# Middle pairs of two feed-forward blocks computed column by token, without transposes of the gated values

## The chip, the cores and the metric

The program runs on one core of one Trainium2 chip. The metric is the device time of one execution in microseconds. Three runs of the kernel before gave 1178.71, 1179.95 and 1180.96 us, median 1179.95. Engines are called by their names: TensorE (PE in the profile), its weight loads (PEld), VectorE (DVE), ScalarE (ACT), GpSimd (POOL) and SyncE (SP, which issues the loads of weights).

## The reference, cut to what matters

256 tokens with 1024 features pass through one hybrid layer (feed-forward, attentions, feed-forward) and then two layers whose norms are modulated by a condition vector. There are four feed-forward blocks, called ffn0 to ffn3 in the kernel; ffn2 and ffn3 belong to the last two layers. All is float32.

```
def swiglu_2(h, w_gate, w_up, w_down):
    return (jax.nn.silu(h @ w_gate) * (h @ w_up)) @ w_down      # 1024 -> 2816 -> 1024

def second_block(...):
    cond = jax.nn.silu(c)
    for i in range(2):
        mod = (cond @ ada_w[i] + ada_b[i])[:, None, :]           # 1024 -> 6 x 1024
        sh1, sc1, g1, sh2, sc2, g2 = jnp.split(mod, 6, axis=-1)
        h = rmsnorm_2(x, norm1_g[i]) * (1.0 + sc1) + sh1
        y = ...attention of layer i...
        x = x + g1 * y
        h = rmsnorm_2(x, norm2_g[i]) * (1.0 + sc2) + sh2
        x = x + g2 * swiglu_2(h, w_gate[i], w_up[i], w_down[i])
    return x
```

## The kernel before

**Precision.** Each float32 matrix is split into a high part (rounded to the type float32r) and a low part (the rest), and each product is three matmuls: high by high, low by high, high by low. ScalarE makes the high part of a weight unit (`hi(u)`, a copy of 128 x 2048), VectorE the low part (`lo(u)`, a subtraction of the same size). The same is done for activations: `h_hi_t` and `h_lo_t` hold the normed input, feature by token, `hid_hi` and `hid_lo` the gated values.

**Weights.** They come in units of 1 MB through a ring of seven slots (`SLOT`, `HELD`); SyncE issues the load of a unit when `unit_done` says that the slot's last user is through. `hi` and `lo` of a unit are issued AHEAD = 4 units before TensorE uses it.

**A feed-forward block.** The 2816 hidden columns are taken in 11 pairs of 256 columns (`PAIRS`). A pair has three units: two for gate and up (part 0 and part 1, four 128-row chunks each, 256 gate columns beside 256 up columns) and one for down. In the kernel before, `gate_up(p, part, t)` keeps 128 tokens of the activations as TensorE's weights and streams 512 columns (gate and up together), so a result is token by column in bank 0 or 1 (`gu_bank`), for t = 0 and 1. ScalarE takes the silu of the gate half (`silu`), VectorE multiplies by the up half (`hidden`). The gated values are then token by column, but the down matmul wants them column by token, so `turn_hid` transposes them (four transposes of 128 x 128 a pair into bank 2), ScalarE copies the high part out of bank 2 (`hid_hi_of`) and VectorE subtracts the low part (`hid_lo_of`). `down_all(p)` adds 24 matmuls of 512 columns to the accumulators in banks 4 to 7. TensorE's order in pair p is: gate and up part 0, transposes of pair p - 1, gate and up part 1, down of pair p - 1, modulation job.

**Modulation.** While the feed-forward blocks run, VectorE also computes the vectors `cond @ ada_w`: one step (`ada(k)`, 128 x 1024) for each of 96 pieces that GpSimd loads, four steps in each of the pairs 2 to 9 of ffn0 to ffn2. The first step of a vector is a plain product. When a vector is complete, a modulation job (`MOD_JOBS`, one half vector a job) sums it over partitions: TensorE transposes it (or multiplies it by ones, for a gate vector, after a split into `acc_hi` and `acc_lo`) into **bank 3**, and VectorE reads bank 3 (`mod_job`, which raises `mod_read`). Jobs stand in pairs 2 to 9 of ffn2 and in pairs 2 and 3 of ffn3. VectorE does its part of the job as the last thing in its pair.

**Order.** Nothing is scheduled by a planner: each engine's instruction list is written by hand in the function `pair` and around it, each engine works through its list in order, and they meet at semaphores. Around the seventh norm (before ffn3) ScalarE's list is: `hi(v0 + 5)`, `hi(v0 + 6)`, then `norm_root(7, 0)`, which squares x of the first 128 tokens and takes the root; VectorE then scales x (`xn`) and TensorE turns it.

Of the kernel before, what the change touches and what calls it, by code (L numbers as in the profile page):

```python
# [6 lines left out]
F32 = mybir.dt.float32  # L7
# [6 lines left out]
P = 128  # L14
# [154 lines left out]

PASS = 4  # L170
# [15 lines left out]
def program(nc, inp, out):  # L186
    with ExitStack() as ctx:
# [12 lines left out]
        h_hi_t = sb("h_hi_t", [P, C, T], F32R)  # L200
        h_lo_t = sb("h_lo_t", [P, C, T], F32R)
# [102 lines left out]
        gu0_done, silu_done, hid_done = sem("gu0_done"), sem("silu_done"), sem("hid_done")  # L304
        hidT_done, hidhi_done, hidlo_done = sem("hidT_done"), sem("hidhi_done"), sem("hidlo_done")
# [34 lines left out]
        def hidT_count(f, p):  # L340

            return (PAIRS + 1) * f + p

# [96 lines left out]
        def _(act):  # L440
# [80 lines left out]
            def ffn(f, n, then):  # L521
# [15 lines left out]
                def hid_hi_of(p, cols, count):  # L537
                    act.wait_ge(hidT_done, count)
                    act.activation(hid_hi[:, p % 2, cols], ps[:, 2, cols], ACT.Copy).then_inc(hidhi_done, 1)  # L539

                def pair(p):
                    ug, ud = ffn_gate(f, p), ffn_down(f, p - 1)
                    if p > 0:
                        hid_hi_of(p - 1, slice(0, 2 * T), hidT_count(f, p - 1) + 1)
                    hi(ug + AHEAD)
                    silu(p, 0)
                    silu(p, 1)
                    hi(ug + 1 + AHEAD)
                    q = gate_of_pair(f * PAIRS + p)
                    if q is not None:  # L550
                        act.wait_ge(ada_used, C * (q + 1))
                        act.activation(acc_hi[:, :], ada_acc[:, q % 2, :], ACT.Copy).then_inc(acc_hi_done, 1)
                    if p > 0:
                        hi(ud + AHEAD)

                u0 = BASE[f"ffn{f}"]
                if f == 0:
                    silu(0, 0)
                    silu(0, 1)
                    hi(3)  # L560
                    act.wait_ge(cond_in, 16)
                    act.activation(cond[:, :], cond[:, :], ACT.Silu).then_inc(cond_ready, 1)
                    hi(4)
                    hi(5)
                    pair(1)
                    late_inputs()
                else:
                    silu(0, 0)
# [7 lines left out]
                    hid_hi_of(0, slice(0, 2 * T), hidT_count(f, 0) + 1)  # L576
                    silu(1, 1)
                    hi(u0 + 3 + AHEAD)
                    hi(u0 + 4 + AHEAD)
                for p in range(2, PAIRS - 1):  # L580
                    pair(p)
# [4 lines left out]
                hid_hi_of(p - 1, slice(0, 2 * T), hidT_count(f, p - 1) + 1)  # L586
                hi(end)
                silu(p, 0)
                hid_hi_of(p, slice(0, T), hidT_count(f, p) + 1)
# [15 lines left out]
                hid_hi_of(p, slice(T, 2 * T), hidT_count(f, p) + 2)  # L605
# [96 lines left out]
            def stick():  # L702
# [110 lines left out]
                hi(v0 + 5)  # L813
                hi(v0 + 6)
                norm_root(7, 0)
# [249 lines left out]
        def _(dve):  # L1065
# [145 lines left out]
            def ffn(f, n, then, factor=None, gated=None):  # L1211
                late = f < 2

                def hidden(p, t):
# [6 lines left out]
                    if p > 1:  # L1221
                        dve.wait_ge(hidT_done, hidT_count(f, p - 2) + 1)
# [15 lines left out]

                def pair(p):
# [9 lines left out]
                    q = gate_of_pair(f * PAIRS + p)  # L1249
                    if q is not None:  # L1250
                        dve.wait_ge(acc_hi_done, GATES.index(q) + 1)
                        V.tensor_tensor(acc_lo[:, :], ada_acc[:, q % 2, :], acc_hi[:, :].bitcast(F32), ALU.subtract) \
                            .then_inc(acc_lo_done, 1)
# [25 lines left out]
                else:  # L1279
# [10 lines left out]
                    lo(u0 + 3 + AHEAD)  # L1290
                    lo(u0 + 4 + AHEAD)
                for p in range(2, PAIRS - 1):
                    pair(p)
# [4 lines left out]
                hid_lo_of(p - 1, slice(0, 2 * T), hidT_count(f, p - 1) + 1)  # L1298
# [532 lines left out]
        def _(pe):  # L1831
# [94 lines left out]
            def ffn(f, n, then):  # L1926
                u0 = BASE[f"ffn{f}"]

                def gate_up(p, part, t, chunks=(0, 1, 2, 3)):
# [4 lines left out]
                    if part == 0 and before is not None:  # L1934
# [12 lines left out]

                def turn_hid(p, tiles):
                    if p == PAIRS - 1 or p == 0:
# [8 lines left out]
                def hi_of(p):  # L1958
                    return lambda k, t: hid_hi[:, p % 2, t * T + k * P:t * T + (k + 1) * P]

                def lo_of(p):
                    return lambda k, t: hid_lo[:, p % 2, t * T + k * P:t * T + (k + 1) * P]

                def down(p, t, h, last=False):
                    return wide_rows([ffn_down(f, p)], t, h, hi_of(p), lo_of(p), [0], p == 0, last)
# [9 lines left out]
                def mod_job(p):  # L1975
# [4 lines left out]
                    wait(pe, mod_read, 2 * q + h)  # L1980
                    if q % 6 in GATE:
# [35 lines left out]
                for p in range(2, PAIRS - 1):  # L2017
                    for t in range(2):
                        gate_up(p, 0, t)
                    turn_hid(p - 1, (0, 1))  # L2020
                    for t in range(2):
                        gate_up(p, 1, t)
# [5 lines left out]
                turn_hid(p - 1, (0, 1))  # L2028
# [549 lines left out]
```

## Time and profile before

| | |
|---|---|
| median of three runs | 1179.95 us (1178.71 to 1180.96) |
| the profiled execution, its own time | 1180.75 us |
| its span, first to last instruction | 1178.9 us |
| TensorE matmuls busy | 1162.7 us, 99% of the span |
| TensorE weight loads busy | 987.2 us, 84% |
| VectorE busy | 814.4 us, 69% |
| ScalarE busy | 599.3 us, 51% |
| GpSimd busy | 51.1 us, 4% |
| mean granted TensorE clock | 1.000 |

The profile's page gives busy time of each engine, the span in 40 slices, the chain of waits that ended last and the costliest groups. Matmuls are pipelined: one begins before the one ahead of it has ended, so their busy times overlap and what a matmul costs is read from start to start. The time of an execution is about 1.9 us more than its span.

### The profile page before, as it was taken

What the parts mean: (1) busy time and instruction counts of PE and PEld (TensorE: products, weight loads), DVE (VectorE), ACT (ScalarE), POOL (GpSimd) and SP (SyncE); (2) the same over time, 40 slices, a digit from 0 to 9 for tenths busy, and PEclk for the clock granted to TensorE, in tenths of its full rate; (3) what the DMA queues carried; (4) which work ended last, traced back from release to release, by engine and by line L of the source; (5) the groups of instructions that cost most, each with busy time, mean ns of one, the idle gap of its engine ahead of it and who ended that gap; (6) DMA issues with size and microseconds to landing.
All of it is one profiled execution on the core that took longest, in us unless ns stands there. A gap on an engine that the chain in (4) does not pass through costs nothing. (4 is left out here: it accounts for less than half of the span.)

```text
span 1178.9 us, 15408 instructions
## 1 busy us (share of the span) xinstructions
PE 1162.7 (99%) x6300; PEld 987.2 (84%) x6300; DVE 814.4 (69%) x1041; ACT 599.3 (51%) x779; POOL 51.1 (4%) x101
## 2 busy tenths in 40 slices
PE   8999999999999999999999999999999999999998
PEld 6888888999999888888878888888889977888887
DVE  5777877435767657887898967778785557554544
ACT  7443356545575643353578544433564775433441
POOL 0011110000000001111000001111000000000000
PEclk9999999999999999999999999999999999999999
DMA  9888694553445478887623457897546304655530
GB/s 369 338 309 318 227 347 165 197 183 139 143 143 177 182 266 318 299 289 282 236 75 140 180 215 280 292 328 278 198 168 222 125 31 185 238 190 179 180 141 36
DMA packets 44422, 253.68 MB, mean 215 GB/s; under 512 B 5568, under 2 KB 5952, under 8 KB 20544
## 3 DMA queue, kind: packets, MB, share of 16 engines
q1 hardware_dynamic: 29088, 199.78, 46.5%
q0 software_dynamic: 13824, 50.34, 12.3%
q10 hardware_dynamic: 1440, 2.58, 0.6%
q8 instruction: 50, 0.82, 0.3%
q14 instruction: 20, 0.16, 0.0%
HBM read 251.63 MB, written 1.05 MB: 214 GB/s over the span
## 5 line engine op out<-in xcount | busy, mean ns | idle before, releaser
L1072 DVE TENSOR_TENSOR w_lo<-raw,w_hi 128x2048 fp32r<-128x2048 f32 x145 | 330.8, 2288 | 114.2 <-ACT w_hi L462 114.2
L462 ACT ACTIVATE w_hi<-raw 128x2048 fp32r<-128x2048 f32 x145 | 275.3, 1910 | 31.9 <-DMA raw<-in_w 31.9
L1844 PE MATMUL ps<-w_hi,h_hi_t 128*128 128x512 f32 (+1 forms) x720 | 284.6, 395 | 1.7 <-DVE w_lo L1072 0.9
L1846 PE MATMUL ps<-w_lo,h_hi_t 128*128 128x512 f32 (+1 forms) x720 | 278.3, 387 | 0.0
L1845 PE MATMUL ps<-w_hi,h_lo_t 128*128 128x512 f32 (+1 forms) x720 | 277.8, 386 | 0.0
L1844 PEld LDWEIGHTS ps<-w_hi,h_hi_t 128*128 128x128 f32 x720 | 135.7, 189 | 28.8 <-DVE w_lo L1072 1.5
L539 ACT ACTIVATE hid_hi<-ps 128x512 fp32r<-128x512 f32 (+1 forms) x48 | 27.0, 562 | 259.8 <-PE ps L1954 259.8
L1846 PEld LDWEIGHTS ps<-w_lo,h_hi_t 128*128 128x128 f32 x720 | 135.4, 188 | 27.9
L1845 PEld LDWEIGHTS ps<-w_hi,h_lo_t 128*128 128x128 f32 x720 | 135.8, 189 | 25.0
L1837 PE MATMUL ps<-h_hi_t,w_hi 128*128 128x256 f32 x400 | 115.0, 288 | 0.0
L1839 PE MATMUL ps<-h_hi_t,w_lo 128*128 128x256 f32 x400 | 113.3, 283 | 0.0
L1838 PE MATMUL ps<-h_lo_t,w_hi 128*128 128x256 f32 x400 | 113.3, 283 | 0.0
L1087 DVE SCALAR_TENSOR_TENSOR ada_acc<-ada_raw,cond,ada_acc 128x1024 f32<-128x1024 f32 x84 | 107.5, 1280 | 2.7 <-DVE ada_acc L1083 0.5
L1072 DVE TENSOR_TENSOR lo_extra<-raw_extra,hi_extra 128x2048 fp32r<-128x2048 f32 x40 | 91.5, 2287 | 13.4 <-ACT hi_extra L462 13.4
L1844 PE MATMUL ps<-w_hi,hid_hi 128*128 128x512 f32 x248 | 96.9, 391 | 0.0
L1846 PE MATMUL ps<-w_lo,hid_hi 128*128 128x512 f32 x248 | 96.6, 390 | 0.0
L1845 PE MATMUL ps<-w_hi,hid_lo 128*128 128x512 f32 x248 | 96.6, 390 | 0.0
L1232 DVE TENSOR_TENSOR hid_lo<-ps,hid_hi 128x512 fp32r<-128x512 f32 (+1 forms) x48 | 31.0, 646 | 90.2 <-ACT hid_hi L539 90.1
L435 POOL DMA_DIRECT2D ada_raw<-in_ada_w x96 | 50.8, 529 | 784.6 <-DVE ada_acc L1087 392.8
L1844 PE MATMUL ps<-hi_extra,h_hi_t 128*128 128x512 f32 x208 | 82.6, 397 | 0.0
L1846 PE MATMUL ps<-lo_extra,h_hi_t 128*128 128x512 f32 x208 | 81.3, 391 | 0.0
L1845 PE MATMUL ps<-hi_extra,h_lo_t 128*128 128x512 f32 x208 | 81.1, 390 | 0.0
(231 smaller groups left out, 1667.7 us busy)
## 6 DMA issues: line engine op xcount, KB each, us to landing
raw<-in_w SPq DMA_DIRECT2D x146, 1024.0 KB, 5.0
ada_raw<-in_ada_w POOLq DMA_DIRECT2D x96, 512.0 KB, 5.3
raw_extra<-in_w SPq DMA_DIRECT2D x40, 1024.0 KB, 5.8
raw<-in_w SPq DMA_DIRECT2D x4, 256.0 KB, 6.1
gate<-in_ada_b ACTq DMA_DIRECT2D x2, 512.0 KB, 12.6
gate<-in_ada_b SPq DMA_DIRECT2D x2, 512.0 KB, 6.0
out_x<-x SPq DMA_DIRECT2D x4, 256.0 KB, 2.0
const<-in_const ACTq DMA_DIRECT2D x1, 768.0 KB, 8.1
```

Of the source, the lines that this page charges most:

```text
L435: pool.dma_start(ada_raw[:, n % ADA_SLOTS, :], w[:, k, (q % 6) * D:(q % 6 + 1) * D]) \
L462: act.activation(w_hi[SLOT[u]], raw[SLOT[u]], ACT.Copy).then_inc(hi_ready, 1)
L539: act.activation(hid_hi[:, p % 2, cols], ps[:, 2, cols], ACT.Copy).then_inc(hidhi_done, 1)
L1072: V.tensor_tensor(w_lo[SLOT[u]], raw[SLOT[u]], w_hi[SLOT[u]].bitcast(F32), ALU.subtract) \
L1087: V.scalar_tensor_tensor(acc, ada_raw[:, n % ADA_SLOTS, :], cond[:, k:k + 1], acc, ALU.mult, ALU.add).then_inc(ada_used, 1)
L1232: V.tensor_tensor(hid_lo[:, p % 2, cols], ps[:, 2, cols], hid_hi[:, p % 2, cols].bitcast(F32), ALU.subtract).then_inc(hidlo_done, 1)
L1837: TE.matmul(dst, wh, x_hi, start=start, stop=False, skip_group_check=True)
L1838: TE.matmul(dst, wh, x_lo, start=False, stop=False, skip_group_check=True)
L1839: return TE.matmul(dst, wl, x_hi, start=False, stop=last, skip_group_check=True)
L1844: TE.matmul(dst, x_hi, wh, start=start, stop=False, skip_group_check=True)
L1845: TE.matmul(dst, x_lo, wh, start=False, stop=False, skip_group_check=True)
L1846: return TE.matmul(dst, x_hi, wl, start=False, stop=last, skip_group_check=True)
```

## The change

Pairs 2 to 9 of ffn2 and ffn3 (`of_columns`) are computed the other way round. `column_pair` on TensorE keeps 128 weight columns as TensorE's weights and streams the activations, so the results are column by token. `h_parts` puts the high and the low part of the activations into one tensor, so one matmul of 512 columns streams both by the high part of the weights: the left half of the bank gets high by high, the right half high by low. A second matmul of 256 columns adds the low part of the weights to the left half. A pair has four column tiles of 128: gate in banks 0 and 1, up in banks 2 and 3.

Each result now stands in two halves that have to be added. ScalarE copies the right halves of two banks to `silu_g` (`gate_low`), VectorE adds the left halves (`gate_sum`), ScalarE takes the silu in place; the same with `hid` for up (`up_low`, `up_sum`), then VectorE multiplies. ScalarE makes `hid_hi` and VectorE `hid_lo` from `hid` directly, already column by token; the transposes and their waits go for these pairs. Bank 3 is now used by the fourth column tile as well as by the modulation jobs, so that tile waits for `mod_read` of the job before. The transposes of pair 1 of both blocks move from inside pair 2 to the middle of `down_all(0)`. Apart from that, ScalarE's `norm_root(7, 0)` moves ahead of `hi(v0 + 6)`.

```
+        def of_columns(f, p):
+            return f >= COLUMNS_FROM and 2 <= p < PAIRS - 1            # COLUMNS_FROM = 2
...
 # ScalarE
+                def column_pair(p):
+                    ug, ud = ffn_gate(f, p), ffn_down(f, p - 1)
+                    hi(ug + AHEAD)
+                    act.wait_ge(gu0_done, f * PAIRS + p + 1)
+                    act.wait_ge(hid_done, hid_count(f, p - 1, 1))
+                    act.activation(silu_g[:, :, :], ps[:, 0:2, T:2 * T], ACT.Copy).then_inc(gate_low, 1)
+                    act.wait_ge(gate_sum, column_count(f, p))
+                    act.activation(silu_g[:, :, :], silu_g[:, :, :], ACT.Silu).then_inc(silu_done, 2)
+                    act.wait_ge(unit_done, ug + 2)
...
+                    act.activation(hid[:, p % 2], ps[:, 2:4, T:2 * T], ACT.Copy).then_inc(up_low, 1)
+                    hi(ug + 1 + AHEAD)
+                    act.wait_ge(hid_done, hid_count(f, p, 1))
+                    act.activation(hid_hi[:, p % 2, :], hid[:, p % 2].rearrange("p k n -> p (k n)"), ACT.Copy) \
+                        .then_inc(hidhi_done, 1)
+                    q = gate_of_pair(f * PAIRS + p)
+                    if q is not None:
...
+                    hi(ud + AHEAD)
...
                 hi(v0 + 5)
+                norm_root(7, 0)
                 hi(v0 + 6)
-                norm_root(7, 0)
...
 # VectorE
+                def part_sum(dst, bank, s):
+                    V.tensor_tensor(dst, dst, ps[:, bank:bank + 2, 0:T], ALU.add).then_inc(s, 1)
...
+                def column_pair(p):
+                    ug, ud = ffn_gate(f, p), ffn_down(f, p - 1)
+                    units = ada_of_pair(f * PAIRS + p)
+                    dve.wait_ge(gate_low, column_count(f, p))
+                    part_sum(silu_g[:, :, :], 0, gate_sum)
+                    lo(ug + AHEAD)
+                    dve.wait_ge(up_low, column_count(f, p))
+                    part_sum(hid[:, p % 2], 2, up_sum)
+                    for k in units[0:1]:
+                        ada(k)
...
+                    V.tensor_tensor(hid[:, p % 2], hid[:, p % 2], silu_g[:, :, :], ALU.mult).then_inc(hid_done, 2)
+                    lo(ug + 1 + AHEAD)
...
+                    modulation(p)
...
 # TensorE
+                def column_pair(p):
+                    for part in range(2):
+                        u = ffn_gate(f, p) + part
+                        pe.wait_ge(lo_ready, u + 1)
+                        for b in range(4):
...
+                            elif part == 0:
+                                pe.wait_ge(gate_sum if b < 2 else up_sum, column_count(f, p - 1))
+                            if part == 0 and b == 3 and f * PAIRS + p - 1 in MOD_JOBS:
+                                q, h = MOD_JOBS[f * PAIRS + p - 1]
+                                pe.wait_ge(mod_read, 2 * q + h + 1)
+                            for c in range(4 * part, 4 * part + 4):
+                                cols = slice((c % 4) * 512 + b * P, (c % 4) * 512 + (b + 1) * P)
+                                TE.matmul(ps[:, b, :].rearrange("p (s n) -> p s n", s=2), w_hi[SLOT[u]][:, cols],
+                                          h_parts[:, :, c, :], start=c == 0, stop=False, skip_group_check=True)
+                                i = TE.matmul(ps[:, b, 0:T], w_lo[SLOT[u]][:, cols], h_hi_t[:, c, :], start=False,
+                                              stop=c == C - 1, skip_group_check=True)
+                            if part == 1 and b == 1:
+                                i.then_inc(gu0_done, 1)
+                        i.then_inc(unit_done, 1)
...
                 def down_all(p):
...
                     for t in range(2):
+                        if t == 1 and p == 0 and of_columns(f, 2):
+                            turn_hid(1, (0, 1))
```

**VectorE, pair 5 of ffn2.** The list before. Line 1232 is the low part of the gated values, 1072 the low part of a weight unit, 1228 the product of the gated values, 1087 a step of the modulation vector, 1098 the read of bank 3.

```order
L1232 TENSOR_TENSOR hid_lo<-ps,hid_hi 128x512 [waits hidhi_done]
L1072 TENSOR_TENSOR w_lo<-raw,w_hi 128x2048 [waits hi_ready]
L1228 TENSOR_TENSOR hid<-silu_g,ps 128x256 [waits hidT_done,silu_done,gu0_done]
L1228 TENSOR_TENSOR hid<-silu_g,ps 128x256 [waits hidT_done,silu_done,unit_done]
L1087 SCALAR_TENSOR_TENSOR ada_acc<-ada_raw,cond,ada_acc 128x1024 [waits ada_used,ada_loaded1]
L1087 SCALAR_TENSOR_TENSOR ada_acc<-ada_raw,cond,ada_acc 128x1024 [waits ada_used,ada_loaded2]
L1072 TENSOR_TENSOR w_lo<-raw,w_hi 128x2048 [waits hi_ready]
L1087 SCALAR_TENSOR_TENSOR ada_acc<-ada_raw,cond,ada_acc 128x1024 [waits ada_used,ada_loaded0]
L1072 TENSOR_TENSOR w_lo<-raw,w_hi 128x2048 [waits hi_ready]
L1087 SCALAR_TENSOR_TENSOR ada_acc<-ada_raw,cond,ada_acc 128x1024 [waits ada_used,ada_loaded1]
L1098 TENSOR_TENSOR gate<-gate,ps 128x512 [waits gate_in0,mod_ps]
```

The same pair now. Lines 1290 are the two sums, 1311 the product, 1316 the low part, 1120 and 1135 the weight unit and the modulation step, 1146 the read of bank 3.

```order
L1290 TENSOR_TENSOR silu_g<-silu_g,ps 128x512 [waits gate_low]
L1120 TENSOR_TENSOR w_lo<-raw,w_hi 128x2048 [waits hi_ready]
L1290 TENSOR_TENSOR hid<-hid,ps 128x512 [waits up_low]
L1135 SCALAR_TENSOR_TENSOR ada_acc<-ada_raw,cond,ada_acc 128x1024 [waits ada_used,ada_loaded1]
L1311 TENSOR_TENSOR hid<-hid,silu_g 128x512 [waits up_sum,silu_done]
L1120 TENSOR_TENSOR w_lo<-raw,w_hi 128x2048 [waits hi_ready]
L1135 SCALAR_TENSOR_TENSOR ada_acc<-ada_raw,cond,ada_acc 128x1024 [waits ada_used,ada_loaded2]
L1316 TENSOR_TENSOR hid_lo<-hid,hid_hi 128x512 [waits hidhi_done]
L1135 SCALAR_TENSOR_TENSOR ada_acc<-ada_raw,cond,ada_acc 128x1024 [waits ada_used,ada_loaded0]
L1120 TENSOR_TENSOR w_lo<-raw,w_hi 128x2048 [waits hi_ready]
L1135 SCALAR_TENSOR_TENSOR ada_acc<-ada_raw,cond,ada_acc 128x1024 [waits ada_used,ada_loaded1]
L1146 TENSOR_TENSOR gate<-gate,ps 128x512 [waits gate_in0,mod_ps]
```

Four 128x512 instructions stand where one of 512 and two of 256 stood. All three weight splits and all four steps now come behind the wait for TensorE's gate tiles (`gate_low`); before, one split came ahead of `gu0_done`. The read of bank 3 is still the last.

**TensorE, pair 5 of ffn2, part 0, now.** Line 2059 is the matmul of both activation parts by the high part of the weights, 2061 the one by the low part. The first row is the last matmul of the third column tile (bank 2), the others belong to the fourth (bank 3).

```order
L2061 MATMUL ps<-h_parts,w_lo 128x256
L2059 MATMUL ps<-h_parts,w_hi 128x512 [waits mod_read,up_sum]
L2061 MATMUL ps<-h_parts,w_lo 128x256
L2059 MATMUL ps<-h_parts,w_hi 128x512
L2061 MATMUL ps<-h_parts,w_lo 128x256
```

Before, the place between part 0 and part 1 of the same pair held the transposes (line 1954), and no gate or up matmul waited for `mod_read`:

```order
L1846 MATMUL ps<-w_lo,h_hi_t 128x512
L1954 MATMUL ps<-const,hid 128x128 [waits hid_done]
L1954 MATMUL ps<-const,hid 128x128
L1954 MATMUL ps<-const,hid 128x128 [waits hid_done]
L1954 MATMUL ps<-const,hid 128x128
L1844 MATMUL ps<-w_hi,h_hi_t 128x512 [waits lo_ready]
```

The transposes are gone from this place, and a wait on VectorE's last instruction of the pair before has come in front of the fourth tile.

## Rows read from the trace of the kernel before

**Rows 1.** The page, part 1: busy us, share of the span, instructions.

```profile
PE 1162.7 (99%) x6300; PEld 987.2 (84%) x6300; DVE 814.4 (69%) x1041; ACT 599.3 (51%) x779; POOL 51.1 (4%) x101
```

**Rows 2.** Busy us by engine (instructions), PEclk, DMA share, GB/s, seven pairs of ffn2.

```profile
706.35:827.37 121.02, 121.02 (x558) 100.08 (x557) 95.30 (x84) 48.40 (x43) 14.79 (x28) 1.00 0.82 294
```

**Rows 3.** The chain of waits in ffn2: start us, us, what.

```profile
706.35 0.44 PE ps L1954 x4
...
827.37 0.44 PE ps L1954 x4
```

**Rows 4.** Timeline of TensorE, pair 7 of ffn2: start us, us, engine, line, operation.

```profile
792.64 0.60 PE L1954 MATMUL ps<-const,hid 128*128 128x128 f32 x4
792.99 0.48 PE L1844 MATMUL ps<-w_hi,h_hi_t 128*128 128x512 f32 x1
793.31 0.40 PE L1845 MATMUL ps<-w_hi,h_lo_t 128*128 128x512 f32 x1
...
795.62 0.39 PE L1846 MATMUL ps<-w_lo,h_hi_t 128*128 128x512 f32 x1
```

**Rows 5.** TensorE with 256 columns: timeline, and weight loads grouped by line.

```profile
329.85 0.28 PE L1839 MATMUL ps<-h_hi_t,w_lo 128*128 128x256 f32 x1
...
331.77 0.28 PE L1837 MATMUL ps<-h_hi_t,w_hi 128*128 128x256 f32 x1
...
L1837 PEld LDWEIGHTS ps<-h_hi_t,w_hi 128*128 128x128 f32 x400 | 76.7, 192 | 2.6 <-issue 2.2 <-ACT qkv L641 0.2
```

**Rows 6.** ScalarE in ffn2 by line; the last number is idle time before.

```profile
L462 ACT ACTIVATE w_hi<-raw 128x2048 fp32r<-128x2048 f32 x24 | 45.4, 1908 | 0.0
```

**Rows 7.** Timeline of ScalarE and VectorE behind the transposes of rows 4.

```profile
793.27 0.60 ACT L539 ACTIVATE hid_hi<-ps 128x512 fp32r<-128x512 f32 x1 [7.80 <-PE ps L1954]
...
796.05 0.38 ACT L534 ACTIVATE silu_g<-ps 128x256 f32<-128x256 f32 x1 [0.37 <-PE ps L1846]
...
793.90 0.69 DVE L1232 TENSOR_TENSOR hid_lo<-ps,hid_hi 128x512 fp32r<-128x512 f32 x1 [1.88 <-ACT hid_hi L539]
```

**Rows 8.** Timeline of ScalarE, VectorE and TensorE around the seventh norm.

```profile
973.87 1.92 ACT L462 ACTIVATE hi_extra<-raw_extra 128x2048 fp32r<-128x2048 f32 x1 [4.07 <-DMA raw_extra<-in_w]
...
979.52 1.04 ACT L478 ACTIVATE junk<-x 128x1024 f32<-128x1024 f32 x1
...
975.46 0.69 DVE L1126 TENSOR_TENSOR x<-x,xn 128x512 f32<-128x512 f32 x1
976.07 2.28 DVE L1072 TENSOR_TENSOR lo_extra<-raw_extra,hi_extra 128x2048 fp32r<-128x2048 f32 x1
...
981.21 0.88 DVE L1141 TENSOR_SCALAR xn<-x,rstd 128x512 f32<-128x512 f32 x2
...
979.68 0.39 PE L1846 MATMUL ps<-w_lo,h_hi_t 128*128 128x512 f32 x1
981.75 0.44 PE L1880 MATMUL ps<-const,xn 128*128 128x128 f32 x2 [1.69 <-DVE xn L1141]
```

**Rows 9.** Timeline of VectorE in ffn2: modulation steps, splits, the read of bank 3.

```profile
747.70 0.75 DVE L1083 TENSOR_SCALAR ada_acc<-ada_raw,cond 128x1024 f32<-128x1024 f32 x1
750.05 1.23 DVE L1252 TENSOR_TENSOR acc_lo<-ada_acc,acc_hi 128x1024 fp32r<-128x1024 f32 x1 [1.61 <-ACT acc_hi L552]
...
802.16 2.28 DVE L1072 TENSOR_TENSOR w_lo<-raw,w_hi 128x2048 fp32r<-128x2048 f32 x1
804.36 1.28 DVE L1087 SCALAR_TENSOR_TENSOR ada_acc<-ada_raw,cond,ada_acc 128x1024 f32<-128x1024 f32 x1
805.56 2.29 DVE L1072 TENSOR_TENSOR w_lo<-raw,w_hi 128x2048 fp32r<-128x2048 f32 x1
...
808.96 0.69 DVE L1102 TENSOR_REDUCE mod<-ps 128x4 f32<-128x512 f32 x1
```

**Rows 10.** Timeline of TensorE, the first weight matmuls of the kernel.

```profile
9.94 0.63 PE L1845 MATMUL ps<-w_hi,h_lo_t 128*128 128x512 f32 x1
10.36 0.60 PE L1846 MATMUL ps<-w_lo,h_hi_t 128*128 128x512 f32 x1
```

More of the change, by code:

```diff
@@ L575, in ffn @@
                     hi(u0 + 2 + AHEAD)
-                    hid_hi_of(0, slice(0, 2 * T), hidT_count(f, 0) + 1)
+                    hid_hi_of(0, slice(0, 2 * T))
                     silu(1, 1)
                     hi(u0 + 3 + AHEAD)
+                    if of_columns(f, 2):
+                        hid_hi_of(1, slice(0, 2 * T))
                     hi(u0 + 4 + AHEAD)
                 for p in range(2, PAIRS - 1):
-                    pair(p)
+                    if of_columns(f, p):
+                        column_pair(p)
+                    else:
+                        pair(p)
                     if f == 1 and p == 7:
@@ L585, in ffn @@
                 end = u0 + FFN_UNITS
-                hid_hi_of(p - 1, slice(0, 2 * T), hidT_count(f, p - 1) + 1)
+                if not of_columns(f, p - 1):
+                    hid_hi_of(p - 1, slice(0, 2 * T))
                 hi(end)
                 silu(p, 0)
-                hid_hi_of(p, slice(0, T), hidT_count(f, p) + 1)
+                hid_hi_of(p, slice(0, T))
                 hi(end + 1)
@@ L1220, in hidden @@
                     dve.wait_ge(silu_done, hid_count(f, p, t))
-                    if p > 1:
-                        dve.wait_ge(hidT_done, hidT_count(f, p - 2) + 1)
+                    if p > 1 and not of_columns(f, p - 2):
+                        dve.wait_ge(hidT_done, turn_count(f, p - 2) + 1)
                     up = ps[:, gu_bank(f, p, t), T:2 * T]
@@ L1248, in pair @@
                         ada(k)
[L1249 to L1253, printed above, removed]
+                    acc_lo_of(p)
                     for k in units[1:2]:
@@ L1290, in ffn @@
                     lo(u0 + 3 + AHEAD)
+                    if of_columns(f, 2):
+                        hid_lo_of(1, slice(0, 2 * T), hidT_count(f, 1) + 1)
                     lo(u0 + 4 + AHEAD)
                 for p in range(2, PAIRS - 1):
-                    pair(p)
+                    if of_columns(f, p):
+                        column_pair(p)
+                    else:
+                        pair(p)
                     if f == 1 and p == 5:
@@ L1297, in ffn @@
                 end = u0 + FFN_UNITS
-                hid_lo_of(p - 1, slice(0, 2 * T), hidT_count(f, p - 1) + 1)
+                if not of_columns(f, p - 1):
+                    hid_lo_of(p - 1, slice(0, 2 * T), hidT_count(f, p - 1) + 1)
                 hidden(p, 0)
@@ L1933, in gate_up @@
                     before = bank_before(f, p, t)
-                    if part == 0 and before is not None:
+                    if part == 0 and of_columns(f, p - 1):
+                        pe.wait_ge(gate_sum, column_count(f, p - 1))
+                    elif part == 0 and before is not None:
                         pe.wait_ge(hid_done, hid_count(f, *before))
@@ L2017, in ffn @@
                 for p in range(2, PAIRS - 1):
[L2018 to L2022, printed above, removed]
+                    if of_columns(f, p):
+                        column_pair(p)
+                    else:
+                        for t in range(2):
+                            gate_up(p, 0, t)
+                        turn_hid(p - 1, (0, 1))
+                        for t in range(2):
+                            gate_up(p, 1, t)
                     down_all(p - 1)
@@ L2027, in ffn @@
                 gate_up(p, 0, 0)
-                turn_hid(p - 1, (0, 1))
+                if not of_columns(f, p - 1):
+                    turn_hid(p - 1, (0, 1))
                 gate_up(p, 1, 0)
```

65 lines of the change are left out of this document (54 added, 11 removed).

## The prediction

> **What bounds the kernel now.** I read the page's busy line first: TensorE is busy 99% of the span, VectorE 69% [rows 1]. That says where to look, not what a change is worth, so I went to the third feed-forward block (the first of the two that the change touches, called ffn2 in the code) and asked for busy times over seven of its pairs. TensorE has no idle time there, VectorE works 95.3 of 121.02 us, ScalarE 48.4, and the granted clock is 1.00 [rows 2]. The chain of waits runs through TensorE alone; from the transposes of one pair to those seven pairs later it takes 827.37 - 706.35 = 121.02 us, 17.29 us a pair [rows 3]. So an instruction taken from TensorE in ffn2 or ffn3 is worth its slot, until TensorE has to wait for somebody. The question is whether it will.
>
> **TensorE's own work.** Ends of matmuls overlap, so I count from start to start. The twelve 512-column matmuls from 792.99 us: after the first, ten steps take 795.62 - 793.31 = 2.31 us, 0.231 each [rows 4]. Over whole pairs it is (17.29 - 2 x 0.44) / 72 = 0.228 us, which I use. A 256-column matmul of the same kind takes (331.77 - 329.85) / 16 = 0.120 us [rows 5]. The four transposes of gated values take 792.99 - 792.64 = 0.35 us, and the first matmul behind them starts its successor 0.09 late (0.32 for 0.23): 0.44 us [rows 4].
> - Before, a pair has 48 matmuls of 512 columns for gate and up: 10.94 us. After, it has 32 of 512 and 32 of 256: 7.30 + 3.84 = 11.14. That is +0.20.
> - The transposes go: -0.44.
> - Sum -0.24 a pair, 16 pairs (2 to 9 of two blocks): -3.9 us if nothing else happens. The mix of both sizes is not in the trace. If every 256 took no longer than half a 512 it would be -0.43 a pair; the other bound is a rival below.
>
> **What the evictions cost.** Per column pair ScalarE gets two copies of 512 elements out of PSUM, a SiLU of 512 and the high part, VectorE two sums, a product and the low part. ScalarE has room (48 of 121 us, and its weight splits never wait for a load [rows 6]). Its 512 form takes 0.60 us and VectorE starts 0.03 after it [rows 7]. VectorE's 512 form takes 0.69 and lets the next start after 0.61 (975.46 to 976.07) [rows 7, 8]; its weight split takes 2.20 from start to start, an adaptive-norm step 1.20 [rows 9], the first step of a vector 0.53 less (0.75 against 1.28) [rows 9]. I price the product and the sums by the 0.61 of the nearest rows; no row shows one that reads and writes only such tiles in this shape, so I let them be half as long or half as long again, which for four instructions is -1.2 or +1.2 us a pair.
>
> **The new wait, which decides.** Before, gate and up use banks 0 and 1, and bank 3 belongs to the modulation. Now the fourth column tile is in bank 3, and in part 0 of a pair it waits for `mod_read` of the pair before. VectorE does that reduction as the last thing of its pair, behind every split and step. Let X be the slot in which TensorE ends gate of pair p (part 1, tile 1).
> - ScalarE starts 0.20 after such an end (796.05 against 795.62 + 0.23) [rows 4, 7]: copy from X + 0.20, VectorE's first sum from X + 0.83. TensorE ends up at X + 2.78, ScalarE's second copy ends at 3.58, before VectorE has finished the sum and one split (3.64), so nothing inside waits.
> - VectorE's list to the end of the reduction is four 512 forms, three splits, four steps, and the reduction: 4 x 0.61 + 3 x 2.20 + 4 x 1.20 + 0.69 = 14.53. So it ends at X + 15.36; where the pair begins a vector (pairs 2, 6, 8) at X + 14.83; in pair 4 (which begins one and splits the gate vector, 1.23 us [rows 9], 1.15 in the list) at X + 15.98.
> - TensorE wants bank 3 at X + 2.78 + 24 x 0.228 (down) + 0.44 (modulation) + 3 x 1.39 (tiles 0 to 2) = X + 12.86. It stands 2.0 to 3.1 us. Queued behind the waiting matmul is all of TensorE, and with it the next gate tile that VectorE needs for its next pair: a loop in which VectorE then idles.
> - From the reduction to the next X: 0.06 to start, 0.11 for the first after a wait, tile 3 1.39, part 1 tiles 0 and 1 2.78: 4.34. The loop is 19.17 us in three pairs, 19.70 in three, 20.32 in one: 136.9 against 121.0 before. Seven pairs hold this wait (3 to 9, each for the one before): **+15.9**. The eighth pair's worth has the -0.24.
> - ffn3 has no steps. Its pair 2 has the gate vector: VectorE's low part of it now comes behind the hidden low part, and its matmuls wait for it. By the same rows it ends at X + 9.5, TensorE is there at 8.25: +1.3, +0.1 to restart. Its reduction is read by X + 12.2 and wanted at 14.1, so bank 3 is free. The other pairs are free: -0.24 x 8 = -1.9. Sum **-0.6**.
> - The transposes of pair 1, moved into the first down, need the gated values 2.7 us after their gate and up; they come about 1 us after (a silu of 0.38 [rows 7] and a product of like size). Bank 2 is wanted for tile 2 of pair 2 at 5.47 + 0.44 + 2.78 = 8.7; the turned values are there at 3.2, and even with a weight split of 1.9 first, the high and low parts end at 6.4. Nothing for both.
>
> **The moved root of the seventh norm.** TensorE's last matmul of the stretch starts at 979.68, so it is ready at 979.91, but the turning of x starts at 981.75: 1.84 us [rows 8]. The square on ScalarE began at 979.52, behind a weight split that had waited for its load; x was ready at 976.15 and ScalarE idle from 975.79 [rows 8]. Now the square starts at 976.2, the norm's product could come 1.69 later (981.21 - 979.52), and VectorE is out of its split at 978.3: ready by 979.0. The wait goes: **-1.8**. What is late next is TensorE itself.
>
> **Sum.** +15.9 - 0.2 - 0.6 - 1.8 = +13.3. The profiled run took 1180.75 us for its span of 1178.9; the median of the three runs is 1179.95. So 1194.0 by the profiled run, 1193.2 by the median: I say 1193.
>
> **Rivals.**
> - Faster, VectorE is in time. If the reduction were read before X + 12.86, only -3.9 and -1.8 would be left: 1174.2. It decides at 2.0 us of VectorE's list. For it: VectorE is busy only 79% now [rows 2], and average load suggests room. Against: three splits and four steps alone are 11.4 us by rows that repeat in every pair, and even half the slot for all four 512 forms gives back 1.2. Chance 8%.
> - The stop slows TensorE. The first matmuls of the kernel are 0.42 apart (9.94, 10.36) against 0.23 [rows 10], which is the lower of the clock's levels, 1.2 GHz, after idle time; but after the 1.84 us stop at 979.91 the rows show no slow stretch. If the seven stops of 2 to 3 us did it, the 4.2 us of matmuls behind each would double: +29, 1222. Chance 3%. The Trainium skill, TensorE: Matmul & The Clock Gate, "Loop structure matters more than you think", warns of the drop to half clock when TensorE waits between bursts; its example is a longer wait than these; if it held for these too, the time would be this rival's.
> - The added weight loads show. A load takes 0.192 [rows 5]; behind a 256 that streams 0.108 (the difference of the two forms, 0.228 and 0.120) 0.084 could stand out, 32 times a pair: +22 in ffn3, about +10 in ffn2, where most of it fills the stop: 1225. Against: those very loads run at one matmul per 0.120. Chance 2%. The Trainium skill (same page, "Measured speedup vs the span model") says a weight load overlaps a running matmul only when the row group differs. Here all groups are full, so by that rule each of the 256 added matmuls would cost its whole load, +49 us; the rows contradict it, since 0.120 is shorter than the load.
> - The forecast, 85%; the rest, 2%, is a time near no change.
>
> **How the numbers follow.** The forecast's own errors: the 512 forms -1.2 to +1.2 a loop, seven loops, gives -8 to +8 at the ends; the nearest rows are closer to the middle. A step that waits for its load would only lengthen the list. So 1186 to 1200 for eight in ten. About 0.2% (2.4 us) is what a measurement here tells from no change: slower 0.90, same 0.02, faster 0.08.
>
> **What would show it.** In the profile after: a period of 19.2 to 20.3 us in ffn2, a TensorE gap of 2 to 3 us before the fourth column tile of pairs 3 to 9, released by VectorE's reduction or gate sum; no such gap in ffn3, with a period of 16.6 (72 x 0.228 + 0.44 = 16.86, less 0.24); one gap of 1.3 us at the gate matmuls of ffn3's pair 2; no gap before the turning of x in norm 7. I am wrong if ffn2 keeps 17.0 us a pair, or if the matmuls behind a gap are 0.42 apart.

## The result, and the profile after

The kernel after takes 1200.46 us, median of four runs (1199.58 to 1202.94), against 1179.9 us for the kernel before (1178.71 to 1180.96): a ratio of 1.0179, 95% interval 1.0164 to 1.0194. It is slower, by 20.6 us where 13 were forecast, and just above the range, which ended at 1200. Its profiled execution took 1199.58 us, with a span of 1197.8 us against 1178.9.

The page of after, busy us with share of the span and instructions, answers to [rows 1]. TensorE is busy 4 us longer in a span 19 us longer, so most of the loss is time in which it stands.

```profile
PE 1166.8 (97%) x6492; PEld 995.9 (83%) x6492; DVE 830.2 (69%) x1057; ACT 616.4 (51%) x795; POOL 51.3 (4%) x101
```

The seven pairs of ffn2, from the start behind the modulation job of pair 2 to that of pair 9, by windows of after (length, then busy us and instructions of PE, PEld, DVE, ACT, POOL, the granted clock, DMA share, GB/s). It answers to [rows 2].

```profile
717.81:858.87 141.06, 126.09 (x644) 106.19 (x642) 101.30 (x92) 55.53 (x51) 14.84 (x28) 0.96 0.74 261
```

And the same seven pairs of before:

```profile
717.91:838.94 121.03, 121.03 (x560) 100.09 (x558) 95.30 (x85) 48.40 (x43) 14.27 (x27) 1.00 0.84 304
```

These seven pairs lose 141.06 - 121.03 = 20.03 us, which is the whole difference of the spans (18.9) and 1 us more. Two things are new in the row: TensorE idles 141.06 - 126.09 = 15 us, and the clock was 0.96 where it had been 1.00. Who makes TensorE wait stands in the list of waits of after, 700 to 860 us (total us, times, longest):

```profile
POOL ada_raw L453 <- DVE ada_acc L1135: 96.8, 25, 11.5
...
PE ps L2059 <- DVE mod L1150: 10.2, 5, 2.4
...
PE ps L2108 <- DVE acc_lo L1296: 2.5, 1, 2.5
PE ps L2059 <- DVE gate L1146: 2.4, 1, 2.4
```

GpSimd's waits are the longest and cost nothing: it waits for room for a load. The three rows of PE are the loss, seven stops in all. Here is the first, on the timeline of TensorE in after (start us, us, what, idle before and releaser):

```profile
722.01 0.28 PE L2061 MATMUL ps<-h_parts,lo_extra 128*128 128x256 f32 x1
...
724.08 0.47 PE L2059 MATMUL ps<-h_parts,hi_extra 128*128 128x512 f32 x1 [1.78 <-DVE mod L1150]
```

And VectorE's whole pair ahead of it, on its own timeline:

```profile
709.96 0.69 DVE L1290 TENSOR_TENSOR silu_g<-silu_g,ps 128x512 f32<-128x512 f32 x1 [7.14 <-ACT silu_g L579]
710.56 2.28 DVE L1120 TENSOR_TENSOR lo_extra<-raw_extra,hi_extra 128x2048 fp32r<-128x2048 f32 x1
712.78 0.69 DVE L1290 TENSOR_TENSOR hid<-hid,ps 128x512 f32<-128x512 f32 x1
713.38 0.75 DVE L1131 TENSOR_SCALAR ada_acc<-ada_raw,cond 128x1024 f32<-128x1024 f32 x1
714.05 0.68 DVE L1311 TENSOR_TENSOR hid<-hid,silu_g 128x512 f32<-128x512 f32 x1
714.65 2.29 DVE L1120 TENSOR_TENSOR w_lo<-raw,w_hi 128x2048 fp32r<-128x2048 f32 x1
716.85 1.28 DVE L1135 SCALAR_TENSOR_TENSOR ada_acc<-ada_raw,cond,ada_acc 128x1024 f32<-128x1024 f32 x1
718.04 0.69 DVE L1316 TENSOR_TENSOR hid_lo<-hid,hid_hi 128x512 fp32r<-128x512 f32 x1
718.65 1.28 DVE L1135 SCALAR_TENSOR_TENSOR ada_acc<-ada_raw,cond,ada_acc 128x1024 f32<-128x1024 f32 x1
719.84 2.29 DVE L1120 TENSOR_TENSOR w_lo<-raw,w_hi 128x2048 fp32r<-128x2048 f32 x1
722.04 1.28 DVE L1135 SCALAR_TENSOR_TENSOR ada_acc<-ada_raw,cond,ada_acc 128x1024 f32<-128x1024 f32 x1
723.24 0.69 DVE L1150 TENSOR_REDUCE mod<-ps 128x4 f32<-128x512 f32 x1
```

The list has no hole, and the reduction is its last entry. The idle time of 7.14 us is ahead of it: VectorE waits for TensorE's gate tiles, and once they are there it has more to do than TensorE has before it wants bank 3. Each waits for the other in turn. The list was put at X + 0.83 to X + 14.83; it takes 723.93 - 709.96 = 13.97, where the forecast had 14.00. TensorE is due 0.12 us after 722.01 and starts at 724.08, a stop of 1.94 us. Measured in this way the seven stops, by the last start before each, are 1.94 (722.01), 2.55 (741.10), 2.62 (ahead of the gate vector's matmul, whose release is at 758.87), 2.51 (782.12), 1.94 (801.95), 2.55 (821.05) and 1.99 us (842.35). Their sum is 16.1 us.

The rest of the 20 us is the clock. Windows of after:

```profile
760.00:765.00 5.00, 5.00 (x21) 4.28 (x21) 3.92 (x3) 0.00 (x0) 1.06 (x2) 0.69 0.71 254
...
820.00:825.00 5.00, 2.61 (x14) 2.03 (x13) 3.73 (x4) 0.00 (x0) 0.92 (x2) 0.96 0.62 193
825.00:830.00 5.00, 5.00 (x23) 4.32 (x22) 0.00 (x0) 0.27 (x1) 0.00 (x0) 0.70 0.81 291
...
845.00:850.00 5.00, 5.00 (x22) 4.27 (x21) 0.00 (x0) 0.00 (x0) 0.00 (x0) 0.66 0.77 268
```

Three of the seven stops, those that end at 758.87, 823.71 and 844.46, are followed by such a stretch; the windows between them, left out here, have 1.00, but for 0.99 in the one from 750 to 760, at whose end the first slow stretch begins. In matmuls it looks like this (timeline of TensorE in after, behind the sixth stop):

```profile
823.71 0.47 PE L2059 MATMUL ps<-h_parts,hi_extra 128*128 128x512 f32 x1 [2.39 <-DVE mod L1150]
824.02 0.28 PE L2061 MATMUL ps<-h_parts,lo_extra 128*128 128x256 f32 x1
824.14 0.40 PE L2059 MATMUL ps<-h_parts,hi_extra 128*128 128x512 f32 x1
824.38 0.28 PE L2061 MATMUL ps<-h_parts,lo_extra 128*128 128x256 f32 x1
824.50 0.54 PE L2059 MATMUL ps<-h_parts,hi_extra 128*128 128x512 f32 x1
824.84 0.41 PE L2061 MATMUL ps<-h_parts,lo_extra 128*128 128x256 f32 x1
825.05 0.63 PE L2059 MATMUL ps<-h_parts,hi_extra 128*128 128x512 f32 x1
```

The first matmuls behind the stop are at full speed (0.24 for a 512, 0.12 for a 256); less than a microsecond later a 512 takes 0.43 and a 256 0.21, the level of 1.2 GHz, as the first matmuls of the kernel did [rows 10]. The Trainium skill (TensorE: Matmul & The Clock Gate, "Loop structure matters more than you think") warns that matmuls with waits between them fall to half clock; its example is a wait of 8 us. The trace agrees for stops of 2 to 2.6 us, but for three of the seven only.

What a fall costs comes out of the periods. The pair that holds the sixth stop takes 21.28 us, between these two starts behind modulation jobs:

```profile
816.86 0.48 PE L2059 MATMUL ps<-h_parts,hi_extra 128*128 128x512 f32 x1
...
838.14 0.48 PE L2059 MATMUL ps<-h_parts,w_hi 128*128 128x512 f32 x1
```

Without any stop a pair of this form takes 17.20 (experiment 5 below); the stop is 2.55 and the matmul behind a stop starts its successor 0.09 late: 19.84. The other 1.44 is the clock's. For the last stop it is 20.73 - 17.20 - 1.99 - 0.09 = 1.45. A stretch at 1.2 GHz lasts 3.4 us here (from 824.6, and at 828.03 a 256 is back at 0.12); a 512 and a 256 take 0.64 us in it for 0.354, so it does 1.9 us of work and loses 1.5. A direct comparison gives a little more: the pair that holds the first stop takes 19.10 us in after (717.81 to 736.91), where no fall follows, and 20.72 in experiment 4 (717.65 to 738.37), where one follows a stop of the same length: 1.6. So a fall costs 1.4 to 1.6 us.

So the seven pairs are 120.6 (the same seven in experiment 5) + 16.1 of stops + 0.6 of late successors + 4.3 of clock = 141.6. The row has 141.06, so the parts are good to some tenths each.

The seventh norm [rows 8] went as worked out. ScalarE and TensorE in after:

```profile
995.65 1.06 ACT L496 ACTIVATE junk<-x 128x1024 f32<-128x1024 f32 x1 [0.49 <-DVE x L1174]
...
997.03 1.90 ACT L480 ACTIVATE w_hi<-raw 128x2048 fp32r<-128x2048 f32 x1
...
999.14 0.39 PE L1936 MATMUL ps<-w_lo,h_parts 128*128 128x512 f32 x1
999.37 1.03 PE L1970 MATMUL ps<-const,xn 128*128 128x128 f32 x8
```

The square now runs ahead of the weight split (997.03), and the turning of x follows the last matmul by 0.23 us, the slot of one matmul: no wait. In ffn3 one stop is left, 1.31 us, ahead of the gate vector's matmul; without it the pairs take 16.8 us, as they did before.

### The profile page after: what moved, and what is told of

Its sections match the earlier page's. It is cut to its first block and busy times, and to the rows that moved or that the text cites. A ratio compares the mean times of both kernels' runs of the same rounds, so it can differ in the third digit from the quotient of the medians.

```text
span 1197.8 us, 15833 instructions
## 1 busy us (share of the span) xinstructions
PE 1166.8 (97%) x6492; PEld 995.9 (83%) x6492; DVE 830.2 (69%) x1057; ACT 616.4 (51%) x795; POOL 51.3 (4%) x101
## 5 line engine op out<-in xcount | busy, mean ns | idle before, releaser
L1934 PE MATMUL ps<-w_hi,h_parts 128*128 128x512 f32 (+1 forms) x536 | 210.8, 393 | 1.9 <-DVE w_lo L1120 0.9
L1936 PE MATMUL ps<-w_lo,h_parts 128*128 128x512 f32 (+1 forms) x536 | 205.9, 384 | 0.0
L1935 PE MATMUL ps<-w_hi,h_parts 128*128 128x512 f32 (+1 forms) x536 | 205.6, 384 | 0.0
L2059 PE MATMUL ps<-h_parts,w_hi 128*128 128x512 f32 x368 | 134.8, 408 | 8.3 <-DVE mod L1150 6.0
L1934 PEld LDWEIGHTS ps<-w_hi,h_parts 128*128 128x128 f32 x536 | 100.8, 188 | 22.3 <-DVE w_lo L1120 1.5
L1936 PEld LDWEIGHTS ps<-w_lo,h_parts 128*128 128x128 f32 x536 | 100.7, 188 | 20.4
L1935 PEld LDWEIGHTS ps<-w_hi,h_parts 128*128 128x128 f32 x536 | 101.0, 188 | 18.1
L1927 PE MATMUL ps<-h_parts,w_hi 128*128 128x256 f32 x400 | 114.9, 287 | 0.0
L1928 PE MATMUL ps<-h_parts,w_hi 128*128 128x256 f32 x400 | 113.1, 283 | 0.0
L1929 PE MATMUL ps<-h_parts,w_lo 128*128 128x256 f32 x400 | 113.1, 283 | 0.0
L2061 PE MATMUL ps<-h_parts,w_lo 128*128 128x256 f32 x368 | 104.9, 285 | 0.0
L2059 PEld LDWEIGHTS ps<-h_parts,w_hi 128*128 128x128 f32 x368 | 71.2, 194 | 26.9 <-issue 9.5
L557 ACT ACTIVATE hid_hi<-ps 128x512 fp32r<-128x512 f32 (+1 forms) x32 | 17.4, 544 | 132.0 <-PE ps L2075 132.0
L1290 DVE TENSOR_TENSOR silu_g<-silu_g,ps 128x512 f32<-128x512 f32 x16 | 11.0, 688 | 103.4 <-ACT silu_g L579 103.4
```

The source lines that it names most:

```text
L1927: TE.matmul(dst, wh, x_hi, start=start, stop=False, skip_group_check=True)
L1928: TE.matmul(dst, wh, x_lo, start=False, stop=False, skip_group_check=True)
L1929: return TE.matmul(dst, wl, x_hi, start=False, stop=last, skip_group_check=True)
L1934: TE.matmul(dst, x_hi, wh, start=start, stop=False, skip_group_check=True)
L1935: TE.matmul(dst, x_lo, wh, start=False, stop=False, skip_group_check=True)
L1936: return TE.matmul(dst, x_hi, wl, start=False, stop=last, skip_group_check=True)
```

## The experiments

Seven kernels. Each was timed beside the kernel before; the ratio is to that.

**1. The bank is read early.** If the stops come from the place of the reduction at the end of VectorE's list, moving it ahead of the last split and step must end six of seven, and with them most of the clock's loss. The gate vector's stops, one in each block, must stay.

```
 column_pair(p), VectorE, after:
                     for k in units[2:3]:
                         ada(k)
+                    modulation(p)
                     lo(ud + AHEAD)
                     ...
-                    modulation(p)
```

> The changed kernel, but in its column pairs VectorE reads bank 3 (the modulation job) before the last weight split and the last adaptive-norm step of the pair, not after them. Theory (the wait of the fourth column tile on that read costs the time): the read ends at most 12.7 us after the end of gate, before TensorE wants bank 3 at 12.9; all stops before the fourth tile go, the two at the gate vector's matmuls (2.6 us in ffn2, 1.3 us in ffn3) stay. Time 1179.9 - 1.8 (norm) + 2.6 + 1.3 = 1182, up to 1.7 more if the clock still falls after the 2.6 us stop. Rival (the time is lost in the added evictions or matmuls, wherever the read stands): near 1200 as the changed kernel.

Measured: 1183.95 us (1182.06 to 1185.63) against 1179.27; ratio 1.0041 [1.0027, 1.0054]. So 16 of the 20.6 us go with the place of one reduction. TensorE's waits from 700 to 860 us in this kernel:

```profile
PE ps L2108 <- DVE acc_lo L1296: 2.4, 1, 2.4
PE ps L1934 <- DVE w_lo L1120: 0.3, 1, 0.3
```

The one stop left in ffn2 is the gate vector's (2.6 us from slot to start), and the clock falls once, behind it (windows of the same kernel). The stop of 1.3 us in ffn3 stays too.

```profile
755.00:760.00 5.00, 3.74 (x14) 3.21 (x15) 5.00 (x4) 1.20 (x1) 0.73 (x2) 0.75 0.87 327
760.00:765.00 5.00, 5.00 (x27) 4.34 (x27) 1.30 (x2) 0.00 (x0) 0.53 (x1) 0.90 0.53 190
```

**2. The moved root alone, in the kernel before.**

```
 before:
                 hi(v0 + 5)
+                norm_root(7, 0)
                 hi(v0 + 6)
-                norm_root(7, 0)
```

> The kernel before with nothing but the root of the seventh norm moved ahead of the weight split. Theory: the 1.84 us stop of TensorE before the turning of x goes whole and nothing else moves: 1178.1 against 1179.9, ratio 0.9985. Rival (the split that is now late takes it back at the start of ffn3): 1179.9, with a new stop of TensorE behind the turning.

Measured over five rounds: 1178.11 us (1177.84 to 1178.69) against 1179.27; ratio 0.9990 [0.9981, 0.9999]. The wait is gone, where [rows 8] had 979.68 and 981.75 (timeline of TensorE in this kernel):

```profile
979.52 0.39 PE L1846 MATMUL ps<-w_lo,h_hi_t 128*128 128x512 f32 x1
979.75 1.03 PE L1880 MATMUL ps<-const,xn 128*128 128x128 f32 x8
```

The mechanism of the -1.8 is right. Its size is less sure: the medians differ by 1.2 us (0.1 to 2.2 by the interval). The spans of the two profiles differ by 2.0 (1176.9 against 1178.9), but the profiled execution of before took 1180.75 us, longer than any of the fifteen that it is timed by here (1178.54 to 1180.13).

**3. The stops filled with matmuls.** To tell the stops from what the clock does after them, TensorE gets work that nothing uses: extra matmuls (two runs of 256 columns) into the bank that the next real matmul clears anyway, 8 or 11 in front of column tile 2, and 11 (ffn2) or 5 (ffn3) in front of the gate vector's matmul (this second place isn't shown). VectorE is as late as before; only TensorE isn't idle.

```
 after, column_pair on TensorE, ahead of the chunks of column tile 2:
+    if part == 0 and b == 2 and f == 2 and 3 <= p and p != 5:
+        for _ in range(8 if p % 2 else 11):
+            TE.matmul(ps[:, 2, :]..., w_hi[SLOT[u]][:, 0:P], h_parts[:, :, 0, :], start=True, stop=True)
```

> The changed kernel with the stops of TensorE filled by matmuls whose results are overwritten: 8 or 11 of 512 columns into bank 2 ahead of the third column tile in the pairs of ffn2 that stop, 11 and 5 into bank 3 ahead of the gate vector's matmuls. The waits and what VectorE has to do stay as they are. Theory (some 6 of the 20.5 us are matmuls at the lower clock after a stop): no matmul is 0.427 us from the next after a stop, mean granted clock 1.000, time 1200.5 - 6 = 1194.5. Rival (the clock's part is elsewhere or nil, the 20.5 are the waits): about 1200, since the waits are the same.

Measured: 1195.69 us (1195.46 to 1195.80), ratio 1.0140 [1.0127, 1.0154]. One wait of 0.2 us is left in ffn2, and the clock is 1.00 (windows of this kernel):

```profile
717.97:855.12 137.15, 136.90 (x712) 115.44 (x710) 101.38 (x92) 55.52 (x51) 14.78 (x28) 1.00 0.76 268
```

It does more work than the kernel after and is 4.8 us faster, 4.6 by the two ratios (0.0039 of 1180). In the profiles the seven pairs are 3.9 us shorter (717.97 to 855.12, 137.15 against 141.06). That is the clock's part, shown by itself, as far as the extra matmuls are just as long as the stops; what is left, 137.15 - 121.03 = 16.1, is the wait's. The spread of the runs shrank too, from 3.4 us to 0.3: after's runs differ in how often the clock fell (mean clock 0.995 in its runs of 1199.6, 0.992 in that of 1202.9).

**4. High and low parts side by side in memory.** In after a 512-column matmul reads two runs of 256, one of the high and one of the low parts, 8 KB apart, and takes 0.236 us where 0.228 had been counted. Is it the two runs?

```
 after:
-    h_parts = sb("h_parts", [P, 2, C, T], F32R)
+    h_parts = sb("h_parts", [P, C, 2, T], F32R)
     ...
-    h_parts[:, :, c, :]
+    h_parts[:, c]
```

> The changed kernel with the high and low parts of the activations stored beside each other per chunk, so that the 512-column matmul streams one run of 512 elements in place of two runs of 256 that lie apart. Theory A (the step from a 512-column to a 256-column matmul takes 0.236 us and not 0.228 because of the two runs): it falls to 0.227, a pair of ffn3 takes 16.5 us and not 16.8, time some 3 us less than the changed kernel, 1197.5. Theory B (it is the change of size, or the weight load behind it): 0.236 and 16.8 stay, time 1200.5.

Measured: 1201.84 us (1200.25 to 1202.87), ratio 1.0192 [1.0178, 1.0206]; nothing is gained. The steps (from a 512 to the 256, and from the 256 to the next 512) stay 0.236 and 0.118 and a column pair of ffn3 stays 16.79 us. The two runs aren't the cause. The time is, if anything, longer because the same stops cost more clock, 0.992 over the span against 0.995; the first stop of ffn2, after which the clock of after stayed up, is followed by the fall here (windows of this kernel):

```profile
715.00:727.00 12.00, 10.21 (x52) 8.52 (x51) 8.93 (x8) 3.85 (x3) 1.58 (x3) 0.92 0.85 309
727.00:755.00 28.00, 25.64 (x127) 21.70 (x126) 17.99 (x17) 10.13 (x11) 2.11 (x4) 0.91 0.66 224
755.00:765.00 10.00, 7.54 (x31) 6.05 (x30) 10.00 (x9) 6.58 (x5) 1.58 (x3) 0.88 0.83 309
...
820.00:830.00 10.00, 7.64 (x38) 6.40 (x37) 6.87 (x7) 1.79 (x1) 1.58 (x3) 0.88 0.52 164
...
840.00:850.00 10.00, 8.21 (x42) 6.83 (x41) 7.65 (x8) 2.58 (x2) 1.58 (x3) 0.90 0.99 403
```

The seven stops of ffn2 are as long as in after to within 0.1 us, but five of them are followed by a fall, not three.

**5. No stops at all.** Experiment 1, and the gate vector's high and low parts made at the head of the pair instead of behind the hidden parts. What is left is TensorE's own work in the new form, the term of -3.9 us.

```
 experiment 1, column_pair, VectorE (ScalarE's copy to acc_hi moves in the same way):
+                    acc_lo_of(p)
                     dve.wait_ge(gate_low, column_count(f, p))
                     part_sum(silu_g[:, :, :], 0, gate_sum)
                     ...
-                    acc_lo_of(p)
```

> As e1_read_early (VectorE reads bank 3 before the last weight split and the last step), and the gate vector's high and low parts are taken at the head of the pair, before the gate copy and the gate sum. Theory: no stop of over 1.3 us of TensorE is left in the changed stretch, clock 1.000; a column pair takes TensorE as long as a pair before (the 0.44 us of transposes gone, 32 steps from 512 to 256 columns at 0.236 and not 0.228 and 32 halves at 0.118 in their place), so what is left is the norm's gain: 1178.1, as e2_root_alone. Rival (column pairs are 0.24 us shorter, as forecast): 1174.3.

Measured over five rounds: 1178.65 us (1178.20 to 1180.96) against 1180.03; ratio 0.9993 [0.9984, 1.0002]. One wait of 0.3 us, on a weight split, is left in ffn2. The span is 1176.9, to a tenth that of experiment 2, and the ratio is 0.0003 above its ratio, 0.4 us. So with the stops gone, sixteen column pairs together gain nothing that shows: the root's gain is all that remains. The timeline of TensorE in ffn3 in this kernel shows why:

```profile
1071.21 0.40 PE L2059 MATMUL ps<-h_parts,w_hi 128*128 128x512 f32 x1
1071.44 0.28 PE L2061 MATMUL ps<-h_parts,w_lo 128*128 128x256 f32 x1
...
1072.27 0.40 PE L2059 MATMUL ps<-h_parts,hi_extra 128*128 128x512 f32 x1
```

A couple is a 512 and the 256 behind it. Three couples take 1072.27 - 1071.21 = 1.06 us, 0.353 each, of which the steps behind a 512 are 0.23 to 0.24. Thirty-two couples make 11.3 us a pair, not the 11.14 of the sum.

**6. The same without alternation.** Experiment 5 with the matmuls of each tile and part in another order: four of 512 columns and then four of 256, a quarter of the changes of size.

```
 experiment 5, column_pair on TensorE:
     for c in range(4 * part, 4 * part + 4):
         TE.matmul(... w_hi ..., h_parts[:, :, c, :], ...)
+    for c in range(4 * part, 4 * part + 4):
         TE.matmul(... w_lo ..., h_parts[:, 0, c, :], ...)
```

> As e5_no_stops, and in each column tile the four 512-column matmuls of a part come first and then its four 256-column ones, in place of alternating. Theory B1 (the 0.009 us belong to each step from 512 to 256 columns): a tile's part takes 3 x 0.227 + 0.236 + 3 x 0.120 + 0.118 = 1.395 us in place of 1.416, 0.17 less a pair, 2.7 us in all: 1175.4, a pair of ffn3 16.62. Rival B2 (the 0.009 us belong to every 512 matmul of this form, whatever follows): pair 16.8 and time as e5_no_stops.

Measured over five rounds: 1176.69 us (1176.33 to 1177.04) against 1180.03; ratio 0.9975 [0.9966, 0.9984]. This is the fastest version, by 0.25% (2.9 us) against before; its span is 1174.8, 2.1 less than in experiment 5. The timeline of TensorE in ffn3 (neighbours of one form are merged, with their count):

```profile
1072.08 1.09 PE L2059 MATMUL ps<-h_parts,hi_extra 128*128 128x512 f32 x4
1073.01 0.63 PE L2063 MATMUL ps<-h_parts,lo_extra 128*128 128x256 f32 x4
1073.48 1.09 PE L2059 MATMUL ps<-h_parts,hi_extra 128*128 128x512 f32 x4
```

Four 512s take 0.93 us (1073.01 - 1072.08), four 256s 0.47: 1.40 for what alternating took 1.41. That is 0.1 us a pair (16.69 against 16.79). Only part of the expected gain came: a 512 takes 0.233 even behind another 512, so it isn't the step from 512 to 256 alone that is long.

**7. Only ffn3 by columns.** After with `COLUMNS_FROM = 3` instead of 2.

```
 after:
-COLUMNS_FROM = 2
+COLUMNS_FROM = 3
```

> The changed kernel with column pairs in ffn3 only (COLUMNS_FROM = 3); ffn2 is as before. Theory (all of the loss is in ffn2; in ffn3 a column pair takes as long as a pair before and only the gate vector's wait of 1.3 us is added; the norm's gain stays): 1179.3 - 1.2 + 1.3 = 1179.4, clock 1.000. Rival (column pairs cost time in themselves, half of the 20.5 us in each block): 1188 or more.

Measured: 1179.59 us (1179.22 to 1180.43) against 1180.03; ratio 1.0000 [0.9991, 1.0009]. All of the loss is in ffn2, the block with modulation steps. One stop is left, the gate vector's (TensorE, this kernel):

```profile
1031.07 0.39 PE L1936 MATMUL ps<-w_lo,hid_hi 128*128 128x512 f32 x1
1032.60 0.47 PE L2108 MATMUL ps<-acc_hi,ones_r 128*128 128x512 f32 x1 [1.15 <-DVE acc_lo L1296]
```

It is 1.53 - 0.23 = 1.3 us long, it isn't followed by a slower clock, and it eats most of the root's gain.

## Why the prediction was off

- **The new wait, right in place, cause and size.** Stops of 2.0 to 3.1 us before the fourth column tile were forecast, released by VectorE's reduction or gate sum; six of 1.94 to 2.55 came there. The seven loops were to take 136.9 us; without the clock's part they take 137.15 (experiment 3). The 512 forms, priced at 0.61 by rows of other instructions, take 0.60 to 0.61 from start to start. Experiment 1 takes the cause away and the stops go.
- **One stop stood elsewhere.** The gate vector's split in ffn2 was put into VectorE's list, but its own reader was not asked for: TensorE's gate matmuls come ahead of the next pair's fourth tile, and stood for it there (2.62 us; 3.1 had been forecast at the bank). In ffn3 the same question was asked and answered rightly, 1.3 forecast and 1.31 measured.
- **The failed step: "the stop slows TensorE", 3%.** The rival was built as all or nothing: all seven stops, a doubling of 4.2 us behind each, +29. The step in it was "after the 1.84 us stop at 979.91 the rows show no slow stretch". One stop of 1.84 us says little on seven that are forecast at up to 3.1, and a rival that holds for some of the stops was not priced. Three of seven stops were followed by a fall, each of 1.4 to 1.6 us: 4.3 to 4.8 us that the sum lacked in ffn2 (3.9 to 4.6 by experiment 3), and most of the error. At even odds for each stop, half of seven times 1.4 would have added 5 us to the sum. The range had room for the 512 forms alone and none for the clock. The prediction's own sign of being wrong, matmuls 0.42 apart behind a gap, did come, behind three of the gaps.
- **The mis-sized term: -0.24 us a pair.** It was -3.9 for sixteen pairs without waits; the measured worth is nothing, or a loss of some tenths (experiment 5 against experiment 2: 0.0 by the spans, 0.4 us more by the ratios, whose intervals reach 1 us to either side). The steps of 0.228 and 0.120 came from stretches of one size only. Alternating, the pair costs 0.353 and not 0.348. Also the period of ffn3 was taken as 16.86 before the change; the trace has 16.80. The prediction said that the mix is not in the trace, and took no other end for it but the rival of the loads. In the sum this is 1.9 in ffn3 and 0.2 in ffn2, where the other seven pairs go by VectorE's loop.
- **The root, -1.8: right in place and cause.** The wait is gone; the gain is 1.2 us by the medians of experiment 2 (0.1 to 2.2), 2.0 by the two profiles.
- **"The added weight loads show" fell.** The 256s among the 512s take 0.12 us though a load takes 0.19. The Trainium skill (TensorE: Matmul & The Clock Gate, "The mechanism" in its part on packing, and not the section that the prediction names) lets a weight load overlap a running matmul only where the row group differs; with all rows in use here, the measurement decides against it.
- **"VectorE is in time" fell** at the place it named: VectorE's list left no idle time in front of the reduction. It needed 2 us, and moving the reduction by two instructions (a split and a step, 2.20 + 1.20) gives 3.4.

Together, in the profiles: 13.3 forecast, + 4.3 for the clock, + 2.1 for the column pairs' own work, - 0.2 for the root is 19.5; the spans differ by 18.9. The medians differ by 20.6. Of the 1.7 between, 0.9 is that after's median lies above its profiled run (the mean clock was 0.992 and 0.994 in two of its four runs, 0.995 in that one), and 0.9 that before's median lies below its own profiled run.

## What to carry to other kernels

Before a buffer gets a second user, look up where in its engine's list the old reader stands: the stop here was not a lack of VectorE's time (without the stops, in experiment 5, it works 101.5 of 120.6 us in the seven pairs) but a matter of order, and moving one reduction two instructions forward took away 16 of the 20.6 us. When TensorE is the bound and a change makes it stand for about 2 us again and again, price the stop and, with a chance for each stop, the slower clock behind it; matmuls that nobody uses can be cheaper than a stop. A matmul's slot read from a stretch of one size isn't its slot among others: a saving of 0.005 us per matmul needs a row of the mix.

## What the runs showed of the hardware

- The granted clock falls behind some short stops and not behind others. In after, of stops of 1.94, 2.55, 2.62, 2.51, 1.94, 2.55 and 1.99 us the third, the sixth and the seventh were followed by a stretch at 1.2 GHz, so the length of a stop alone doesn't decide; in experiment 4 the same stops, to 0.1 us, were followed by five falls. The stop of 1.3 us in ffn3 never was (after and experiments 1, 4 and 7, one each). A fall costs 1.4 to 1.6 us. What decides is open.
- The slower stretch begins late: behind the stop that ended at 823.71 the matmuls kept full speed until 824.50; behind the gate vector's stop of experiment 1, which ended at 756.26, until 757.50.
- Matmuls of 512 columns take 0.228 to 0.236 us from start to start in the first ten or so after a change of size, and 0.226 to 0.227 later. It shows in before as well: [rows 4] has 0.231 on average right behind transposes, where whole pairs give less. Experiment 4 excludes the layout of the streamed operand and experiment 6 that only the step from 512 to 256 is long; the cause is open.
